# Operands in PSUM, deeper rings of u tiles, and the gates' writes on ScalarE's queue, in a hybrid decoder block

## The reference

```python
def peer(h, w_q, sub_keys, u_tab, v_tab):
    q = (h @ w_q).reshape(B, T, PEER_HEADS, 2, PEER_HALF)          # 8 heads, 2 x 128
    s = jnp.einsum('bthpd,hpnd->bthpn', q, sub_keys)               # 128 keys per half
    v1, i1 = lax.top_k(s[..., 0, :], K); v2, i2 = lax.top_k(s[..., 1, :], K)   # K = 16
    cand = (v1[..., :, None] + v2[..., None, :]).reshape(B, T, PEER_HEADS, K * K)
    cidx = (i1[..., :, None] * PEER_NKEYS + i2[..., None, :]).reshape(B, T, PEER_HEADS, K * K)
    top_s, pos = lax.top_k(cand, K)
    eidx = jnp.take_along_axis(cidx, pos, axis=-1)
    gates = jax.nn.softmax(top_s, axis=-1)
    # per token, over its 128 experts e of 16384:
    act = gelu(h . u_tab[e]);  out += gate[e] * act * v_tab[e]
```

## Time and profile before

| | |
|---|---|
| median of 3 runs | 2072.36 us (2067.4 to 2073.57) |
| the profiled execution's own time | 2071.39 us |
| its span, first to last instruction | 2069.6 us |
| PE busy | 1843.4 us, 89% |
| PEld busy | 1612.1 us, 78% |
| DVE busy | 1457.7 us, 70% |
| POOL busy | 808.8 us, 39% |
| ACT busy | 708.7 us, 34% |
| mean granted TensorE clock | 0.94 |
| DMA | 432.19 MB, mean 209 GB/s |

### The profile page before, as it was taken

How to read it: one execution, slowest core, us unless ns; L and a number is a source line. 1 busy time by engine, 2 the same in 40 slices (tenths; PEclk the granted TensorE clock), 3 DMA queues, 4 the chain that set the end, 5 groups by cost and what they waited for, 6 DMA issues and landing times. The chain is left out here.

```text
span 2069.6 us, 31925 instructions
## 1 busy us (share of the span) xinstructions
PE 1843.4 (89%) x11421; PEld 1612.1 (78%) x11421; DVE 1457.7 (70%) x2844; ACT 708.7 (34%) x1059; POOL 808.8 (39%) x443
## 2 busy tenths in 40 slices
PE   1898988879996998999998889876999999999997
PEld 1576677768875777998987888876999888888886
DVE  5896344452323478999997888875678788777776
ACT  3432222233324323333323344332333333333333
POOL 1333311123432346888884222222345444333330
PEclk8999977779998999999999999998999999999999
DMA  8364000012322225887875888887889999988883
GB/s 320 126 213 151 30 2 0 0 41 74 99 82 77 75 92 195 263 269 250 267 251 185 256 260 265 269 274 232 284 294 325 343 366 373 342 314 322 322 324 129
DMA packets 178085, 432.19 MB, mean 209 GB/s; under 512 B 15176, under 2 KB 91080, under 8 KB 177888
## 3 DMA queue, kind: packets, MB, share of 16 engines
q1 hardware_dynamic: 125600, 274.52, 39.3%
q0 software_dynamic: 36864, 134.23, 18.9%
q10 hardware_dynamic: 15552, 22.55, 2.9%
HBM read 383.54 MB, written 47.71 MB: 208 GB/s over the span
## 5 line engine op out<-in xcount | busy, mean ns | idle before, releaser
L188 POOL DMA_INDIRECT own_rows<-in_peer_v_dram,own_row x128 | 214.9, 1679 | 328.2 <-DVE y_own L1803 309.5
L188 POOL DMA_INDIRECT own_rows<-in_u_rows_dram,own_row x128 | 193.7, 1513 | 302.5 <-DVE own_rows L1531 229.7
L1713 PE MATMUL bank<-v_hi,coef_lo 128*128 128x512 f32 x768 | 299.2, 390 | 0.0
L1713 PE MATMUL bank<-v_lo,coef_hi 128*128 128x512 f32 x768 | 299.2, 390 | 0.0
L1713 PE MATMUL bank<-v_hi,coef_hi 128*128 128x512 f32 x768 | 298.8, 389 | 0.1
L1183 PE MATMUL bank<-h_hi,piece_hi 128*128 128x384 f32 (+1 forms) x672 | 240.9, 358 | 32.4 <-POOL piece_lo L1320 28.0
L1320 POOL TENSOR_TENSOR piece_lo<-piece,piece_hi 128x1024 fp32r<-128x1024 f32 x84 | 212.1, 2525 | 131.7 <-ACT piece_hi L1250 130.9
L1183 PE MATMUL bank<-h_lo,piece_hi 128*128 128x384 f32 (+1 forms) x672 | 236.0, 351 | 0.0
L1183 PE MATMUL bank<-h_hi,piece_lo 128*128 128x384 f32 (+1 forms) x672 | 235.8, 351 | 0.0
L1250 ACT ACTIVATE piece_hi<-piece 128x1024 fp32r<-128x1024 f32 x84 | 89.1, 1061 | 285.2 <-PE bank L1183 207.0
L1788 DVE TENSOR_TENSOR v_lo<-v_tile,v_hi 128x1024 fp32r<-128x1024 f32 x128 | 156.4, 1222 | 24.6 <-ACT v_hi L1744 22.5
(11 more groups left out here) (344 smaller groups left out, 4034.3 us busy)
## 6 DMA issues: line engine op xcount, KB each, us to landing
v_tile<-in_peer_v_dram SPq DMA_DIRECT2D x128, 512.0 KB, 5.2
piece<-in_peer_u_dram SPq DMA_DIRECT2D x68, 512.0 KB, 4.3
ada<-in_w_ada_dram SPq DMA_DIRECT2D x48, 512.0 KB, 5.0
gate_scratch<-gate_block SPq DMA_DIRECT2D x12, 2048.0 KB, 11.8
gate_tiles<-gate_scratch SPq DMA_DIRECT2D x32, 768.0 KB, 6.8
gelu_scratch<-gelu_early ACTq DMA_DIRECT2D x104, 192.0 KB, 3.8
gelu<-gelu_scratch SPq DMA_DIRECT2D x104, 192.0 KB, 5.7
u_early<-in_peer_u_dram SPq DMA_DIRECT2D x36, 512.0 KB, 7.9
```

Of the source, the lines that this page charges most:

```text
L188: pool.indirect_dma_start(own_rows[:, n % R], None, tables[n // NS], bass.IndirectOffsetOnAxis(ap=own_row[:, n % NS:n % NS + 1], axis=0)). ...
L1713: last = nc.tensor.matmul(y_bank(t, half)[:], w[:, j, t * P:(t + 1) * P], x[:, j, c], start=(first and n == 0), stop=(final and n == 2))
```

## The change

1. `bank` 6 and 7 become one PSUM tensor `bank_pair`; L1463 reads h from it (`h_psum`), not from `h_own`. `h_own` is still written, for the later stages.
2. The key numbers as floats `fi`, the ranks `abf`, `ab`, `ab_eq` and the scores `score` move from SBUF into PSUM banks 4 and 5 (`look`, `score`). The rank arithmetic is put in another order so that no instruction has two PSUM inputs: the remainder is now a product and sum behind a wait for "shift", and three tiles stay in SBUF (`ab_in`). `shift` first copies each head's largest score to SBUF ("gmax").
3. The early pieces go to banks 0 and 1 (the first two wait for ScalarE's copies of the last queries), the closing transposes to banks 2 to 4.
4. Retrieval: `w` is the expert stage's `v_tile` with WR = 4 slots, `w_hi` and `w_lo` get HR = 3 slots. ScalarE splits three pieces at the start and piece n+3 when piece n is done. GpSimd runs `rest` for 21 pieces before the fetches. The keys still stand behind piece 1 in SyncE's queue.
5. Gates stage: `w` gets 3 slots (the split tiles keep 2). The 2 MB writes are issued by ScalarE, right behind its copies of units 3 and 7 and a wait for them, and ScalarE waits for the last ones at the end.

```diff
-        bank = [top.enter_context(nc.psum_tensor(f"bank{i}", [P, 512], F32)) for i in range(8)]
+        bank = [top.enter_context(nc.psum_tensor(f"bank{i}", [P, 512], F32)) for i in range(6)]
+        bank_pair = top.enter_context(nc.psum_tensor("bank_pair", [P, D], F32))
+        bank += [bank_pair[:, 512 * n:512 * n + 512] for n in range(2)]
...
+    h_psum = g_["bank_pair"]
+    look = bank[4][:].rearrange("p (x n t k) -> p x n t k", x=4, n=2, t=TT)
+    fi, abf, ab, ab_eq = look[:, 0], look[:, 1], look[:, 2, 0].bitcast(U32), look[:, 2, 1]
+    score = bank[5][:].rearrange("p (t h k) -> p t h k", t=TT, h=PH)
...
+    WR, HR = G, 3
...
-        w = sb(ctx, "piece", [P, 2, KT, P])
-        w_hi = sb(ctx, "piece_hi", [P, 2, KT, P], F32R)
-        w_lo = sb(ctx, "piece_lo", [P, 2, KT, P], F32R)
+        w = g_["v_tile"][:].rearrange("p n (k m) -> p n k m", k=KT)
+        w_hi = sb(ctx, "piece_hi", [P, HR, KT, P], F32R)
+        w_lo = sb(ctx, "piece_lo", [P, HR, KT, P], F32R)
...
-                for n in range(2):
+                for n in range(WR):
                     sp.dma_start(w[:, n], source(n)).then_inc(s_w[n], 16)
-                sp.dma_start(keys[:], a["sub_keys"]).then_inc(s_k, 16)
-                for n in range(2, NPIECE):
-                    sp.wait_ge(lo_ready, n - 1)
-                    sp.dma_start(w[:, n % 2], source(n)).then_inc(s_w[n % 2], 16)
+                    if n == 1:
+                        sp.dma_start(keys[:], a["sub_keys"]).then_inc(s_k, 16)
+                for n in range(WR, NPIECE):
+                    sp.wait_ge(lo_ready, n - WR + 1)
+                    sp.dma_start(w[:, n % WR], source(n)).then_inc(s_w[n % WR], 16)
...
-                for n in range(2):
+                for n in range(HR):
                     split(n)
...
-                for n in range(B0 + 2):
+                for n in range(B0 + HR):
                     rest(n)
...
                     nc.vector.tensor_scalar(a_, pos[:, S], 3, None, ALU.logical_shift_right).then_inc(*V.step("shift"))
-                    nc.vector.tensor_scalar(r_, pos[:, S], 7, None, ALU.bitwise_and).then_inc(*V.step("mask"))
+                    dve.wait_ge(*at("shift"))
+                    nc.vector.scalar_tensor_tensor(r_, a_, -8.0, pos[:, S], ALU.mult, ALU.add).then_inc(*V.step("mask"))
...
-                        nc.vector.scalar_tensor_tensor(rows[:, i % R], rows[:, i % R], 1.0, h_own[:], ALU.mult, ALU.mult,
+                        nc.vector.scalar_tensor_tensor(rows[:, i % R], rows[:, i % R], 1.0, h_psum[:], ALU.mult, ALU.mult,
...
+    WR = 3
...
+                        if u % UB == UB - 1:
+                            act.wait_ge(*A.after(f"unit{u}", i))
+                            act.dma_start(spill[:, :, bass.ds(i * SLOTS + slot, 1)].rearrange("p g o j t -> p (g o) j t"),
+                                          block_g[:, slot].rearrange("p (g j) t -> p g j t", j=4)).then_inc(stored[slot], 16)
...
-                            if more or m + 2 < U_ITER:
+                            if more or m + WR < U_ITER:
                                 sp.wait_ge(lo_ready, i * U_ITER + (m + 1))
-                                sp.dma_start(w[:, m % 2], a["peer_u"][i * U_ITER + (N_RETR + m + 2)]).then_inc(s_w[m % 2], 16)
-                        if u % UB == UB - 1:
-                            slot = u // UB
-                            sp.wait_ge(*A.after(f"unit{u}", i))
-                            sp.dma_start(spill[:, :, bass.ds(i * SLOTS + slot, 1)].rearrange("p g o j t -> p (g o) j t"), block_g[:, slot].rearrange("p (g j) t -> p g j t", j=4)).then_inc(stored[slot], 16)
-
-                for m in range(2):
+                                sp.dma_start(w[:, m % WR], a["peer_u"][i * U_ITER + (N_RETR + m + WR)]).then_inc(s_w[m % WR], 16)
+
+                for m in range(WR):
                     sp.dma_start(w[:, m], a["peer_u"][N_RETR + m]).then_inc(s_w[m], 16)
```

More of the change, by code:

```diff
@@ L1119, in retrieve_stage @@
         pos = sb(ctx, "top_at", [P, TT, TOPK], U32)
[L1120 to L1122 removed]
+        ab_in = sb(ctx, "top_ab_in", [P, 3, TT, TOPK])
         hot = sb(ctx, "rank_hot", [P, 2, TT, K2])
[L1124 removed]
         sel = sb(ctx, "key_all", [P, 2, TT, PH, TOPK])
@@ L1127, in retrieve_stage @@
         gsum = sb(ctx, "gate_sum", [P, 2, TT, PH])
-        s_w = [sem(ctx, f"piece_landed{i}") for i in range(2)]
+        s_w = [sem(ctx, f"piece_landed{i}") for i in range(WR)]
         stored = [sem(ctx, f"gelu_stored{i}") for i in range(2)]
@@ L1139, in steps @@
             n += ["key", "cand_a", "cand_b", "cand_c"] + [f"{x}{t}" for x in ("cmax", "cat", "crest", "cmax2_", "cat2_") for t in ts_]
-            return n + ["score", "shift", "mask", "row9", "row1", "i_row", "j_rest", "i_all", "j_all", "hot0", "hot1", "pick0", "pick1", "sel0", "sel1"]
+            return n + ["score", "shift", "mask", "row1", "i_row", "row9", "j_rest", "i_all", "j_all", "hot0", "hot1", "pick0", "pick1", "sel0", "sel1"]
         pre_v = ["scale_p", "scale2"] + [f"xn{t}" for t in range(TT)] + [f"lo{k}" for k in range(KT)]
-        own_v = ["gsub", "own_f", "own_row", "gsum", "grec", "own_gate", "h_own"]
-        post_v = ["gsub", "gsum", "grec", "gates", "idx0", "idx1", "gT"]
+        own_v = ["gmax", "gsub", "own_f", "own_row", "gsum", "grec", "own_gate", "h_own"]
+        post_v = ["gmax", "gsub", "gsum", "grec", "gates", "idx0", "idx1", "gT"]
         sv = sem(ctx, "rt_vector")
@@ L1182, in product @@
                         for m, (ww, x) in enumerate(((w_hi, h_hi), (w_hi, h_lo), (w_lo, h_hi))):
-                            last = nc.tensor.matmul(out, ww[:, n % 2, k, :], x[:, k, 0:nt], start=(k == 0 and m == 0), stop=(k == KT - 1 and m == 2))
+                            last = nc.tensor.matmul(out, ww[:, n % HR, k, :], x[:, k, 0:nt], start=(k == 0 and m == 0), stop=(k == KT - 1 and m == 2))
                     last.then_inc(piece_done, 1)
@@ L1190, in early @@
                         pe.wait_ge(gelu_done, e - 1)
-                    product(n, bank[4 + e % 2][:, 0:TD], TD)
+                    else:
+                        pe.wait_ge(q_ready, NQ - 1 + e)
+                    product(n, bank[e % 2][:, 0:TD], TD)
                 def own_scores(h):
@@ L1241, in _ @@
                         src = (sel[:, n, t] if n < 2 else gates[:, t]).rearrange("p h k -> p (h k)")
-                        last = nc.tensor.transpose(bank[n][:, t * P:(t + 1) * P], src, C["ident"])
+                        last = nc.tensor.transpose(bank[2 + n][:, t * P:(t + 1) * P], src, C["ident"])
                     last.then_inc(turned, 1)
@@ L1255, in early @@
                     act.wait_ge(piece_done, n + 1)
-                    if n + 2 < NPIECE:
-                        split(n + 2)
+                    if n + HR < NPIECE:
+                        split(n + HR)
                     if e >= 2:
                         act.wait_ge(stored[e % 2], 16 * (e // 2))
-                    nc.scalar.activation(gel[:, e % 2, :], bank[4 + e % 2][:, 0:TD], ACT.Gelu).then_inc(gelu_done, 1)
+                    nc.scalar.activation(gel[:, e % 2, :], bank[e % 2][:, 0:TD], ACT.Gelu).then_inc(gelu_done, 1)
                     act.wait_ge(gelu_done, e + 1)
@@ L1331, in _ @@
                         n += 1
-                    if B0 + 2 + m < NPIECE:
-                        rest(B0 + 2 + m)
+                    if B0 + HR + m < NPIECE:
+                        rest(B0 + HR + m)
             @block.vector
@@ L1443, in shift @@
                     g, sc, n = gates[:, t0:t1], score[:, t0:t1], (t1 - t0) * PH
-                    nc.vector.tensor_tensor(th(g), th(sc), th(sc)[:, :, 0:1].to_broadcast([P, n, TOPK]), ALU.subtract).then_inc(*V.step("gsub"))
+                    top = gsum[:, 1, t0:t1].rearrange("p t h -> p (t h)")
+                    nc.vector.tensor_copy(top, th(sc)[:, :, 0]).then_inc(*V.step("gmax"))
+                    dve.wait_ge(*V.after("gmax"))
+                    nc.vector.tensor_tensor(th(g), th(sc), top.unsqueeze(2).to_broadcast([P, n, TOPK]), ALU.subtract).then_inc(*V.step("gsub"))
                 dve.wait_ge(*VA.after("sel1", PH - 1))
@@ L1454, in _ @@
                 for n in range(2):
-                    last = nc.vector.tensor_copy(h_own[:, 512 * n:512 * n + 512], bank[6 + n][:])
+                    last = nc.vector.tensor_copy(h_own[:, 512 * n:512 * n + 512], h_psum[:, 512 * n:512 * n + 512])
                 last.then_inc(*VO.step("h_own"))
@@ L1500, in scatter_stage @@
         gel = sb(ctx, "gelu_early2", [P, 2, TD])
-        s_w = [sem(ctx, f"u_early_landed{i}") for i in range(2)]
+        s_w = [sem(ctx, f"u_early_landed{i}") for i in range(WR)]
         s_gel = [sem(ctx, f"gelu2_stored{i}") for i in range(2)]
@@ L1598, in _ @@
                     act.wait_ge(s, 16 * (NR * U_ITER // 2 + 1))
+                for s in stored:
+                    act.wait_ge(s, 16 * (NR + 1))
             @block.sync
@@ L1622, in _ @@
                 body(NR - 1, False)
```

(2 more changed lines are left out.)

33 lines of the change are left out of this document (14 added, 19 removed).

## The result

The changed kernel takes 1993.48 us in the median (1992.23 to 1996.61, 4 runs) against 2072.41 for the kernel before, measured beside it: 0.9626 of the time, 95% interval 0.9607 to 0.9645. The gain is 79 us where the prediction had 64. The profiled execution took 1992.23 us, its span 1990.4.

A forecast was written before the change was run, and what follows sets the result against it. VectorE, held by GpSimd, was taken to bound the retrieval heads, and SyncE's queue to cause the gates' waits. 2071.4 - 27.5 (retrieval) - 36 (gates) = 2007.9, say 2008 us; range 1990 to 2038.

The forecast's parts named there:

- the whole excess of 9.8 us per head: Retrieval heads: VectorE's time beyond its operations' best durations, standing behind GpSimd; all 9.8 us per head were to go.
- Part 1: Retrieval heads: operands in PSUM cut VectorE from 39.0 to 31.1 us per head; TensorE then bounds at 34.7.
- Part 2: Retrieval: deeper rings cost 4 us at the start and gain at the turn; retrieval in all -27.5 us.
- The start cost: Retrieval start: third split, waiting for piece 2 behind the keys, stands ahead of h_raw; +4 us, bounds 0 and 5.5.
- the turn: Retrieval, queries to u tiles: piece 20 stands ahead of GpSimd's fetches, piece 21 behind them; piece 22 near 814.
- The reserve of 4 us for small waits: Retrieval, over its remaining pieces: 4 us kept for small waits that remain.
- Part 3: Gates stage: SyncE only loads, three deep, removing up to 45.5 us of VectorE's waits; -36 us, bounds -45 and -14.
- the reserve of 9.6 us for late loads: Gates stage: loads late at 97% DMA share, 0.6 us in each of 11 half-rounds and 3 in the last round.
- (a): Retrieval and gates: all cover holds, both better bounds, -34 and -45, 1992 us; chance 0.15.
- (b): Gates stage: DMA bandwidth replaces the queue's wait, holding 87%; gates gain only 14, 2030 us; chance 0.17.
- (c): Retrieval heads: PSUM operands don't free VectorE, heads stay near 39 us, 2032 us; chance 0.08.
- (d): Gates stage: ScalarE blocks behind its own write when issuing the gelu store; at worst 2106 us; chance 0.05.

The follow-up runs named there:

- e3: The changed kernel with both gates-stage parts undone (two u slots, 2 MB writes on SyncE): 2039.15 us.
- e5: The changed kernel with all retrieval operands (h, score, keys, digits) in SBUF again, deeper rings and gates part kept: 2036.93 us.
- e4: The changed kernel with only the row product reading h from SBUF again; score, keys and digits stay in PSUM: 1990.42 us.
- e7: The changed kernel with the keys' load behind the third piece and TensorE's wait for it moved to the first scores: 1993.16 us, single run.
- e9: The changed kernel with two orders changed at the turn to u tiles, and the third piece split behind the h loop at the start: 1982.15 us.
- e12: The changed kernel with 1 MB more, used by nobody, loaded in each of ten gates half-rounds: 1997.78 us.
- e11: The changed kernel with 0.5 MB more, used by nobody, loaded in each of ten gates half-rounds: 1995.62 us.

## Why the prediction was right, and where its terms were off

**The reading.** Right: VectorE was held by GpSimd, and SyncE's queue made the gates' waits; e3, e5 and the durations after show both. Not needed: that the whole excess of 9.8 us per head goes. I had 3.6 of its 7.9 us hidden behind TensorE; e4 keeps more than half of the excess and loses nothing.

**Part 1.** The mechanism was right; VectorE's sum, 31.1 per head, was too high, harmlessly: it is busy in 30.5 of 40 us, 26.4 per head of 34.64. One term of it was the price of PSUM, and these rows show none: L1476 has a mean of 1.214 us where I had 1.28. I had taken L1077's shorter product as the measure of a fixed cost. The larger part is that I took 39.0 us per head as work, where VectorE also idled, and left the blocked small operations out of the 9.8. TensorE's 34.7 per head, the term that set the result, was 34.64. The Trainium skill's rule (SBUF — State Buffer, "Who interferes with whom"), that a VectorE instruction with at most one SBUF input doesn't contend with GpSimd, agrees with the trace: with h in PSUM L1476 takes 1.214 us in the mean, with h in SBUF 1.844 (e4).

**Part 2.** The start cost, +4, was 3.9, by the mechanism named, as e7 and e9 show. Piece 22 came at 814.11 where I had 814, but the stage had begun 2.1 us earlier: the turn was 2.2 us worse than said. Piece 19's 2.92 us behind gsub was not in my steps, and after the wait before piece 21 the step to piece 22 took 6.80 instead of 5.5, since the first 2.69 us ran at the lower clock, which my steps didn't have. The reserve of 4 us for small waits was not needed, and pieces took 4.16, not 4.18. So -30.1 against -27.5. The unused reserve and the dearer turn partly cancel.

**Part 3** has the large error: -45.6 against -36. The step that failed is the reserve of 9.6 us for late loads. VectorE's waits on the split fell from 46.9 to 1.4 us, by 45.5, and the stage by 45.6: no load was late enough to count. The reserve rested on the sentence that a DMA share of 97% "is more than any stage of this kernel shows". That came from one average, 0.87 over 425 us of the expert stage. A stretch inside it, of the kernel before, reads:

```profile
1650.00:1750.00 100.00, 100.00 (x443) 82.81 (x442) 85.82 (x104) 38.39 (x52) 40.63 (x25) 1.00 0.99 371
```

371 GB/s with TensorE at 100.00 of 100 us: before the change the trace already held a stretch that spoke against the reserve, though with other transfers in it. e12 shows it in the gates stage itself.

Between the two profiled executions the gain is 79.2 us, 15.7 more than the 63.5 of the sum. Of these 9.6 are this reserve and 2.6 the retrieval. The other 3.5 are the stretches that the change doesn't touch, 2.1 before it and 1.4 behind it: luck, and not mechanism.

**The rivals.** (a) came nearest: 1992. All cover held in the heads and in the gates, while the start cost of 3.9 us stayed and the turn cost 2.2 us more than said. (b) falls by e11 and e12. (c) falls by L1416 and L1476; its figure of 2032 is close to e5's 2036.9 by chance, where the operands are in SBUF and the blocking stays. (d) falls: the store behind a write took 0.34 to 2.36 us, about the 1 to 3 us of the prediction, and ScalarE's idle time covered it. But one took 7.82, past the 3 us that I had named as a sign of being wrong. It cost nothing here, but e11 and e12 show (d)'s mechanism at work: behind holds of 11.45 and 13.10 us TensorE waits 3.52 and 3.96 us.

## What to carry to other kernels

Read a resource's share over short stretches before it is called near its limit: an average over a stage can hide the stretch that speaks against it. Where two parts of a change remove the same wait, their gains don't add: the queue's move alone did what queue and ring did. A wait of TensorE can cost more than its length, where the granted clock behind it is lower. An engine that is "busy" while it stands behind another has spare time that no busy share shows, and spare time counts only where nothing downstream waits for what lies behind it.
